# Half 0's attention in a hybrid decoder layer: values as weights, transposed probabilities streamed, division before the transposes, output collected by head pairs

## The chip, the cores and the metric

One Trainium2 chip, one NeuronCore. The metric is the device time of one execution in microseconds (us). The engines are called PE (TensorE's matmuls) and PEld (its weight loads), DVE (VectorE), ACT (ScalarE), POOL (GpSimd) and SP (SyncE). They run their own queues in order and meet at semaphores.

## The reference

One decoder layer over 1024 tokens of width 1024, all float32: a half-step SwiGLU FFN, a token mixer, a cross-attention to 256 memory tokens, and a second half-step FFN, each between two RMS norms. The mixer projects h with one matrix and has two head groups: a gated DeltaNet (4 heads of 128) and a dilated sliding-window attention (8 heads of 64). The change is in the latter:

```python
def dilated_mixer(q, k, v):
    qh, kh, vh = heads(q), heads(k), heads(v)
    slopes = 2.0 ** (-8.0 * jnp.arange(1, SWA_HEADS + 1, dtype=jnp.float32) / SWA_HEADS)
    for window, dilation in ((128, 1), (512, 4), (2048, 16)):
        o_i, lse_i = dilated_branch(qh, kh, vh, slopes, window, dilation)   # causal softmax(q k^T / 8 + alibi) v
        ...
    wts = jax.nn.softmax(jnp.stack(lses, axis=0), axis=0)
    o = jnp.einsum("gbhs,gbhsd->bhsd", wts, jnp.stack(outs, axis=0))
```

The three branches are merged by their softmax denominators. So for the first 512 tokens it is one causal softmax over at most 512 keys, if each key's score gets, beside its slope times distance, the logarithm of the number of branches that see it. The kernel does just that: the bias is made once and kept in DRAM.

## The kernel before, in words

The kernel works on two halves of 512 tokens (h is 0 or 1), each of TT = 4 tiles of P = 128 tokens. Activations are kept with channels on partitions. Every large product is made of three fp32r matmuls (high parts, and two cross terms with a low part), 128 x 128 weights against 512 columns; the high part is rounded by ACT (w_hi, line 2022), the low part subtracted by DVE (w_lo, line 2666), and SP streams raw weight blocks into a ring of three.

The order of the work is written out by hand. Each engine has a main program (the large products and what belongs to them) and a side job, a generator. After every few main matmuls PE calls `tick()`, which runs the side job's next step; the other engines call theirs at the corresponding places. Half 0's side job while its projections and the second FFN-down stage run is `mixer(0)`: its DeltaNet, and after that its attention. `MIXER[h]` is the list of its steps, the same for all engines.

Half 0's attention has UNITS = 32 units, u = 4 * head + i for query tile i. A unit has i + 1 key tiles, so the widths are 128, 256, 384 and 512. The step "att", u does on each engine:

- PE: `p_transposed(u)`, i + 1 transposes of the probabilities into the PSUM bank SB[2]; then `pv(u - 1)`, the product with the values into SB[3]; then `qk(u + 2)`, the scores into SB[0] or SB[1]. These are fp32 (the scores fp32r); an fp32 matmul shows as two records, a transpose as one.
- DVE: `smax(u + 2)`, scores plus bias and their row maximum (line 3220), the negative maximum (3227); then `fin(u - 1)`: the reciprocal of the row sum (3239) and the scaled copy of the product from SB[3] to `onat` (3241).
- ACT: `exp(u + 1)` with the row sum (2434), and `pt_copy(u)`, the transposed probabilities from SB[2] to SBUF.
- POOL: loads of queries, keys, values and biases, two heads or head pairs ahead.

`prob_of(n)` and `pt_of(n)` are rings of two. In `pv` the transposed probabilities (128 keys x 128 queries) are the stationary weights and the values (128 keys x 64) are streamed; the result has queries on partitions, in one of two places of SB[3], so `pv(u)` waits for the copy of the unit before (`out_sbuf`). The output projection needs channels on partitions. For that there is a step "pair" after every eighth unit: PE transposes the four 128 x 128 tiles of a head pair from `onat` into SB[2] (line 1837), ACT copies them to `qbT` (2479), and `p_transposed` of the following units waits for that copy (`outT_sbuf`). Two steps "conv" at the end split the DeltaNet's and the attention's output into hb_hi (ACT, 2490 and 2495) and hb_lo (DVE, 3322) for the output projection (1429 to 1431).

Main matmuls in this stretch are at lines 1561 to 1563 (`long_rows`), four accumulators A[0..3] that ACT (2055) and DVE (2703) copy out at its end. Elsewhere: 1400 to 1402 `cgran`; 1378 and 1379 `cgran_ab`, the 16 gate columns; 1724 and 1738 DeltaNet products.

Of the kernel before, what the change touches and what calls it, by code (L numbers as in the profile page):

```python
# [17 lines left out]
ACT = mybir.ActivationFunctionType  # L18
# [245 lines left out]
def hybrid_layer(nc, t):  # L264

    ctx = ExitStack()
    with ctx:
# [161 lines left out]
        def norm_ticks(r, q):  # L429
# [66 lines left out]
            "distance", "log_count", "qk_in0", "qk_in1", "v_in0", "v_in1", "bias_in0", "bias_in1", "scores", "max",  # L496
            "neg_max", "probs", "pT_psum", "pT_sbuf", "out_psum", "out_sbuf", "outT_psum", "outT_sbuf",
            "k_class", "stat_out", "stat_in", "merge_diff", "merge_exp", "out_merged", "outT_sum")}
# [841 lines left out]
        def _(pe):  # L1340
# [288 lines left out]
            def mixer(h):  # L1629
# [144 lines left out]
                def p_transposed(u):  # L1774
                    n = h * UNITS + u
                    nk = TT if h else u % TT + 1
                    pe.wait_ge(attn["probs"], n + 1)
                    if n:
                        pe.wait_ge(attn["pT_sbuf"], n)
                    if h and merged_before(u):  # L1780
                        pe.wait_ge(attn["outT_sum"], merged_before(u))
                    elif h == 0 and u >= 9:
                        pe.wait_ge(attn["outT_sbuf"], (u - 1) // 8)
                    for c in range(nk):
                        tr = pe.transpose(SB[2][:, c * P:(c + 1) * P], prob_of(n)[:, c * P:(c + 1) * P], ident[:])
                    tr.then_inc(attn["pT_psum"], 1)

                def pv(u):
                    hd, i = u // TT, u % TT
                    n = h * UNITS + u  # L1790
                    p = hd // 2
                    ch = slice((hd % 2) * AD, (hd % 2 + 1) * AD)
                    if u >= 1:
                        pe.wait_ge(attn["out_sbuf"], n)
                    pe.wait_ge(attn["pT_sbuf"], n + 1)
                    if u % 8 == 0:
                        pe.wait_ge(attn["v_in0"] if p % 2 == 0 else attn["v_in1"], 32 * h + (64 if h else 16) * (p // 2 + 1))
                    if h == 0:
                        groups = [[v_ring(h, p)[:, c, ch] for c in range(i + 1)]]
                    else:  # L1800
                        groups = [[v_ring(h, p)[:, i + c, ch] for c in range(2)], [vs_ring(p)[:, c, i, ch] for c in range(2)]]
                    for a, values in enumerate(groups):
                        for c, v in enumerate(values):
                            mm = pe.matmul(SB[3][:, out_cols(n, a)], pt_of(n)[:, (2 * a + c) * P:(2 * a + c + 1) * P], v,  # L1804
                                           start=(c == 0), stop=(c == len(values) - 1))
                    mm.then_inc(attn["out_psum"], 1)

                for what, l, k in MIXER[h]:
# [14 lines left out]
                    elif what == "att":  # L1823
# [5 lines left out]
                        if u + 2 < UNITS:  # L1829
                            if u == -2:  # L1830
                                pe.wait_ge(delta["gated"], (h + 1) * TT)
                            qk(u + 2)
                    elif what == "pair":
                        pe.wait_ge(attn["out_sbuf"], 8 * (l + 1))
                        pe.wait_ge(attn["pT_sbuf"], min(8 * (l + 1), UNITS - 1) + 1)
                        for i in range(TT):
                            tr = pe.transpose(SB[2][:, i * P:(i + 1) * P], onat_of(l)[:, 0, i, :], ident[:])
                        tr.then_inc(attn["outT_psum"], 1)
                    elif what == "merge" and k >= 2:
                        if k == 2:  # L1840
                            pe.wait_ge(attn["out_merged"], l + 1)
                            pe.wait_ge(attn["pT_sbuf"], UNITS + min(8 * l + 15, UNITS))
                        else:
                            pe.wait_ge(attn["outT_sbuf"], AH // 2 + l + 1)
                        for i in range(TT):
                            tr = pe.transpose(SB[2][:, i * P:(i + 1) * P], onat_of(l)[:, k - 2, i, :], ident[:])
                        tr.then_inc(attn["outT_psum"], 1)
# [144 lines left out]
        def _(act):  # L1992
# [393 lines left out]
            def mixer(h):  # L2386
# [62 lines left out]
                for what, l, k in MIXER[h]:  # L2449
# [27 lines left out]
                    elif what == "pair":  # L2477
                        act.wait_ge(attn["outT_psum"], l + 1)
                        act.activation(qbT[:, l, :], SB[2][:], ACT.Copy).then_inc(attn["outT_sbuf"], 1)
                    elif what == "merge" and k == 0:  # L2480
                        act.wait_ge(attn["merge_diff"], l + 1)
                        act.activation(sm[:, 2:4, :], sm[:, 2:4, :], ACT.Exp).then_inc(attn["merge_exp"], 1)
                    elif what == "merge" and k == 2:
                        act.wait_ge(attn["outT_psum"], AH // 2 + 2 * l + 1)
                        act.activation(qbT[:, l, :], SB[2][:], ACT.Copy).then_inc(attn["outT_sbuf"], 1)
# [145 lines left out]
        def _(dve):  # L2631
# [468 lines left out]
            def mixer(h):  # L3100
# [106 lines left out]
                def smax(u):  # L3207
# [18 lines left out]
                    else:  # L3226
                        dve.tensor_scalar(sm[:, 19, n % 2:n % 2 + 1], mx[:, 0:1], -(AD ** -0.5), None, ALU.mult).then_inc(attn["neg_max"], 1)

                def fin(u):
                    n = h * UNITS + u  # L3230
                    hd, i = u // TT, u % TT
                    ch = slice((hd % 2) * AD, (hd % 2 + 1) * AD)
                    if h:
                        both_parts = SB[3][:, 256 * (n % 2):256 * (n % 2) + 2 * AD].rearrange("p (a d) -> p a d", a=2)
                        dve.wait_ge(attn["out_psum"], n + 1)
                        dve.tensor_copy(onat_of(hd // 2)[:, :, i, ch], both_parts).then_inc(attn["out_sbuf"], 1)
                        return
                    dve.wait_ge(attn["probs"], n + 1)
                    link(dve.reciprocal(sm[:, 22, n % 4:n % 4 + 1], sm[:, 20, n % 4:n % 4 + 1]))
                    dve.wait_ge(attn["out_psum"], n + 1)  # L3240
                    dve.tensor_scalar(onat_of(hd // 2)[:, 0, i, ch], SB[3][:, out_cols(n)],
                                      sm[:, 22, n % 4:n % 4 + 1], None, ALU.mult).then_inc(attn["out_sbuf"], 1)

                def merge(p, k):
# [9 lines left out]
                    elif k == 1:  # L3254
# [6 lines left out]
                        parts = onat_of(p).rearrange("p a i (h d) -> p (a i h) d", h=2)  # L3261
                        dve.wait_ge(attn["out_sbuf"], UNITS + 8 * (p + 1))
                        dve.tensor_tensor(parts, parts, e_own.unsqueeze(2).to_broadcast([P, 4 * TT, AD]), ALU.mult).then_inc(attn["out_merged"], 1)
                    elif k == 3:
                        dve.wait_ge(attn["outT_psum"], AH // 2 + 2 * p + 2)
                        dve.wait_ge(attn["outT_sbuf"], AH // 2 + p + 1)
# [3 lines left out]
                for what, l, k in MIXER[h]:  # L3270
# [40 lines left out]
                    elif what == "att":  # L3311
                        u = l
                        if u + 2 < UNITS:
                            smax(u + 2)
                        if u >= 1:
                            fin(u - 1)
# [194 lines left out]
```

## Time and profile before

| what | us |
|---|---|
| median of 3 runs | 2397.37 (2395.45 to 2398.05) |
| the profiled execution | 2398.63 |
| its span, first to last instruction | 2396.8 |
| PE busy | 2352.7 (98%) |
| DVE / ACT / POOL busy | 1407.6 (59%) / 1059.5 (44%) / 513.3 (21%) |
| granted clock of PE, mean | 0.996 |

Busy time says how long an engine had an instruction in it; for PE ends are modelled and neighbours overlap, so the distance from one start to the next is what an instruction costs. An engine's idle time is given with what ended it. Half 0's attention runs from 931 to 1027 us of the span.

### The profile page before, as it was taken

The page shows a single profiled execution, that of the slowest core. Times are in us where ns is not written, and L with a number is a line of the kernel's source. Part 1 is how long each engine was busy: PE and PEld are TensorE (multiplying, and loading weights), DVE is VectorE, ACT ScalarE, POOL GpSimd, SP SyncE. Part 2 cuts the span into 40 slices and gives each one's busy share as a digit, 9 for nine tenths or more (in the row PEclk, how much of TensorE's full clock was granted, in tenths as well). Part 3 has the DMA queues.
Part 4 walks back from the last instruction along what each step waited for, and adds up shares of the span by engine and source line. Part 5 has one row for each costly group of instructions (what it writes and reads, how often), then busy time and mean ns, then how long its engine had stood idle before and what let it go on. Part 6 is the DMA issues. An engine that isn't in the chain of part 4 may idle for free.

```text
span 2396.8 us, 36179 instructions
## 1 busy us (share of the span) xinstructions
PE 2352.7 (98%) x14220; PEld 1974.5 (82%) x14220; DVE 1407.6 (59%) x2431; ACT 1059.5 (44%) x1860; POOL 513.3 (21%) x661
## 2 busy tenths in 40 slices
PE   8999999999999999999999999999999999999997
PEld 7788888888877778888788777888888888899986
DVE  6766666534676654469755565455463536799722
ACT  7544444324443323555434443686253433466511
POOL 3030000062004333222213332331020113223201
PEclk9999999999999999999999999999999999999999
DMA  8533333584533458754344432663342344644652
GB/s 270 152 107 106 118 111 106 213 296 131 167 80 98 159 199 268 210 166 125 83 124 137 125 96 63 169 166 114 103 149 88 95 144 152 207 150 150 227 214 87
DMA packets 319080, 355.19 MB, mean 148 GB/s; under 512 B 16448, under 2 KB 237888, under 8 KB 318656
## 3 DMA queue, kind: packets, MB, share of 16 engines
q1 hardware_dynamic: 282016, 264.34, 34.8%
q0 software_dynamic: 35712, 88.28, 12.1%
q8 instruction: 114, 1.87, 0.3%
q14 instruction: 54, 0.44, 0.1%
q10 hardware_dynamic: 1184, 0.27, 0.1%
HBM read 284.61 MB, written 68.22 MB: 147 GB/s over the span
## 4 chain that ended last, share of the span: by engine, by line
PE 91%; DVE 3%; ACT 2%; issue 1%; DMA 1%; POOL 1%; SPq 0%; DVEq 0%; ACTq 0%; POOLq 0%
PE acc L1400 9%; PE acc L1402 9%; PE acc L1401 9%; PE acc L1472 7%; PE acc L1473 7%; PE acc L1474 7%; PE acc L1429 5%; PE acc L1431 5%; PE acc L1430 5%; PE acc L1561 2%; PE side L1804 2%; PE acc L1563 2%; PE acc L1562 2%; PE side L1619 1%; PE side L1862 1%
## 5 line engine op out<-in xcount | busy, mean ns | idle before, releaser
L2666 DVE TENSOR_TENSOR w_lo<-w_raw,w_hi 128x1024 fp32r<-128x1024 f32 x276 | 344.9, 1250 | 350.8 <-ACT w_hi L2022 346.9
L2022 ACT ACTIVATE w_hi<-w_raw 128x1024 fp32r<-128x1024 f32 x276 | 291.6, 1057 | 335.2 <-PE acc L1431 100.9
L1400 PE MATMUL acc<-ha_hi,w_hi 128*128 128x512 f32 x800 | 323.3, 404 | 0.6 <-DVE w_lo L2666 0.6
L1402 PE MATMUL acc<-ha_hi,w_lo 128*128 128x512 f32 x800 | 313.5, 392 | 0.0
L1401 PE MATMUL acc<-ha_lo,w_hi 128*128 128x512 f32 x800 | 312.7, 391 | 0.0
L1402 PEld LDWEIGHTS acc<-ha_hi,w_lo 128*128 128x128 f32 x800 | 150.5, 188 | 32.5
L1400 PEld LDWEIGHTS acc<-ha_hi,w_hi 128*128 128x128 f32 x800 | 150.7, 188 | 29.7 <-DVE w_lo L2666 1.0
L1401 PEld LDWEIGHTS acc<-ha_lo,w_hi 128*128 128x128 f32 x800 | 150.9, 189 | 28.1
L2737 DVE TENSOR_TENSOR st_w<-st_raw,st_w 128x512 fp32r<-128x512 f32 x175 | 136.3, 793 | 54.4 <-ACT st_w L2107 53.5
L2107 ACT ACTIVATE st_w<-st_raw 128x512 fp32r<-128x512 f32 x175 | 109.4, 625 | 37.0 <-PE acc L1474 32.1
L1474 PE MATMUL acc<-s_hi,st_w 128*128 128x512 f32 x288 | 112.0, 389 | 0.0
L1473 PE MATMUL acc<-s_lo,st_w 128*128 128x512 f32 x288 | 112.0, 389 | 0.0
L1472 PE MATMUL acc<-s_hi,st_w 128*128 128x512 f32 x288 | 112.0, 389 | 0.0
L3220 DVE CUSTOM_DVE_ANT_0 arena<-side,arena 128x256 f32<-128x256 f32 (+2 forms) x96 | 40.3, 445 | 91.7 <-PE side L1771 49.9
L1118 POOL TENSOR_TENSOR arena<-arena,m_lvl 128x512 f32<-128x512 f32 x48 | 71.3, 1492 | 91.2 <-PE side L1699 79.3
L2107 ACT ACTIVATE st_w<-st_t 128x512 fp32r<-128x512 f32 x70 | 44.2, 632 | 99.9 <-PE acc L1474 59.6
L1472 PE MATMUL acc<-hb_hi,st_w 128*128 128x256 f32 (+1 forms) x276 | 87.0, 315 | 0.8 <-DVE part L2782 0.3
L1473 PE MATMUL acc<-hb_lo,st_w 128*128 128x256 f32 (+1 forms) x276 | 85.7, 311 | 0.0
L1474 PE MATMUL acc<-hb_hi,st_w 128*128 128x256 f32 (+1 forms) x276 | 85.7, 310 | 0.0
L2782 DVE TENSOR_TENSOR part<-acc,part 128x512 f32<-128x512 f32 (+1 forms) x105 | 58.4, 557 | 41.5 <-PE acc L1474 41.5
L1400 PE MATMUL acc<-hb_hi,w_hi 128*128 128x512 f32 x208 | 81.3, 391 | 0.0
L1402 PE MATMUL acc<-hb_hi,w_lo 128*128 128x512 f32 x208 | 81.0, 389 | 0.0
(529 smaller groups left out, 6073.7 us busy)
## 6 DMA issues: line engine op xcount, KB each, us to landing
act_in<-act_dram SPq DMA_DIRECT2D x88, 512.0 KB, 5.1
w_raw<-in_ffn_w_down SPq DMA_DIRECT2D x86, 512.0 KB, 3.9
act_dram<-act_out SPq DMA_DIRECT2D x66, 512.0 KB, 2.6
w_raw<-in_w_in SPq DMA_DIRECT2D x56, 512.0 KB, 3.8
w_raw<-in_ffn_w_gate SPq DMA_DIRECT2D x35, 512.0 KB, 3.8
w_raw<-in_ffn_w_up SPq DMA_DIRECT2D x35, 512.0 KB, 4.1
st_raw<-in_ffn_w_gate SPq DMA_DIRECT2D x35, 512.0 KB, 3.8
st_raw<-in_ffn_w_up SPq DMA_DIRECT2D x35, 512.0 KB, 4.9
```

Source lines behind the costliest of these rows:

```text
L1400: pe.matmul(out, hi[:, k, 0:m], xh[:, k, 0:n], start=(k == 0), stop=False)
L1401: pe.matmul(out, hi[:, k, 0:m], xl[:, k, 0:n], start=False, stop=False)
L1402: done = pe.matmul(out, lo[:, k, 0:m], xh[:, k, 0:n], start=False, stop=(k == KT - 1))
L1429: pe.matmul(out, xh[:, kk, ts], hi[:, k, :], start=(kk == 0), stop=False)
L1430: pe.matmul(out, xl[:, kk, ts], hi[:, k, :], start=False, stop=False)
L1472: pe.matmul(out, hi[:, ws], xh, start=(opens and k == 0), stop=False, skip_group_check=not opens)
L1473: pe.matmul(out, hi[:, ws], xl, start=False, stop=False, skip_group_check=not opens)
L1474: done = pe.matmul(out, lo[:, ws], xh, start=False, stop=(k == TT - 1), skip_group_check=not opens)
L2022: act.activation(hi_at(j), raw_at(j), ACT.Copy).then_inc(w_hi_ok, 1)
L2107: act.activation(st_slot(q, 0), st_source(q), ACT.Copy).then_inc(st_hi, 1)
L2666: dve.tensor_tensor(lo_at(j), raw_at(j), hi_at(j).bitcast(F32), ALU.subtract).then_inc(w_lo_ok, 1)
L2737: dve.tensor_tensor(st_slot(q, 1), st_source(q), st_slot(q, 0).bitcast(F32), ALU.subtract).then_inc(st_lo, 1)
```

## The change

For half 0 only, five things.

1. `pv`: the values (128 keys x 64 channels of the head) are the stationary weights, the transposed probabilities are streamed, and the result has channels on partitions: `SB[3][ch, i * P:(i + 1) * P]`, where ch is partitions 0 to 63 for an even head and 64 to 127 for an odd one. The eight units of a head pair fill SB[3] in the layout that `qbT` wants.
2. A row sum is now along the streamed axis, so the division comes earlier: DVE's `norm_probs(u + 1)` scales the probability row in place, ahead of `smax(u + 2)`, and `p_transposed` waits for `probs_normed`.
3. `fin` is gone in half 0, and with it the wait of `pv` for `out_sbuf`.
4. The four transposes of each step "pair" are gone; ACT copies SB[3] to `qbT` as soon as `pv` has done eight units. The step itself stays in the list.
5. The wait for that copy moves from `p_transposed` to the first `pv` of the next head pair, which overwrites SB[3].

Half 1 keeps its form; only its semaphore counts change.

```diff
                 def p_transposed(u):
                     n = h * UNITS + u
                     nk = TT if h else u % TT + 1
-                    pe.wait_ge(attn["probs"], n + 1)
+                    pe.wait_ge(attn["probs"] if h else attn["probs_normed"], n + 1)
                     if n:
                         pe.wait_ge(attn["pT_sbuf"], n)
                     if h and merged_before(u):
                         pe.wait_ge(attn["outT_sum"], merged_before(u))
-                    elif h == 0 and u >= 9:
-                        pe.wait_ge(attn["outT_sbuf"], (u - 1) // 8)
...
-                    if u >= 1:
-                        pe.wait_ge(attn["out_sbuf"], n)
+                    if h and u >= 1:
+                        pe.wait_ge(attn["out_sbuf"], u)
+                    if h == 0 and u >= 8 and u % 8 == 0:
+                        pe.wait_ge(attn["outT_sbuf"], u // 8)
                     pe.wait_ge(attn["pT_sbuf"], n + 1)
...
                     if h == 0:
-                        groups = [[v_ring(h, p)[:, c, ch] for c in range(i + 1)]]
-                    else:
-                        groups = [[v_ring(h, p)[:, i + c, ch] for c in range(2)], [vs_ring(p)[:, c, i, ch] for c in range(2)]]
+                        for c in range(i + 1):
+                            mm = pe.matmul(SB[3][ch, i * P:(i + 1) * P], v_ring(h, p)[:, c, ch], pt_of(n)[:, c * P:(c + 1) * P],
+                                           start=(c == 0), stop=(c == i))
+                        mm.then_inc(attn["out_psum"], 1)
+                        return
+                    groups = [[v_ring(h, p)[:, i + c, ch] for c in range(2)], [vs_ring(p)[:, c, i, ch] for c in range(2)]]
...
-                    elif what == "pair":
-                        pe.wait_ge(attn["out_sbuf"], 8 * (l + 1))
-                        pe.wait_ge(attn["pT_sbuf"], min(8 * (l + 1), UNITS - 1) + 1)
-                        for i in range(TT):
-                            tr = pe.transpose(SB[2][:, i * P:(i + 1) * P], onat_of(l)[:, 0, i, :], ident[:])
-                        tr.then_inc(attn["outT_psum"], 1)
...
                     elif what == "pair":
-                        act.wait_ge(attn["outT_psum"], l + 1)
-                        act.activation(qbT[:, l, :], SB[2][:], ACT.Copy).then_inc(attn["outT_sbuf"], 1)
+                        act.wait_ge(attn["out_psum"], 8 * (l + 1))
+                        act.activation(qbT[:, l, :], SB[3][:], ACT.Copy).then_inc(attn["outT_sbuf"], 1)
...
+                def norm_probs(u):
+                    dve.wait_ge(attn["probs"], u + 1)
+                    link(dve.reciprocal(sm[:, 22, u % 4:u % 4 + 1], sm[:, 20, u % 4:u % 4 + 1]))
+                    pb = prob_of(u)[:, 0:(u % TT + 1) * P]
+                    dve.tensor_scalar(pb, pb, sm[:, 22, u % 4:u % 4 + 1], None, ALU.mult).then_inc(attn["probs_normed"], 1)
+
...
-                    dve.wait_ge(attn["probs"], n + 1)
-                    link(dve.reciprocal(sm[:, 22, n % 4:n % 4 + 1], sm[:, 20, n % 4:n % 4 + 1]))
                     dve.wait_ge(attn["out_psum"], n + 1)
-                    dve.tensor_scalar(onat_of(hd // 2)[:, 0, i, ch], SB[3][:, out_cols(n)],
-                                      sm[:, 22, n % 4:n % 4 + 1], None, ALU.mult).then_inc(attn["out_sbuf"], 1)
...
                         u = l
+                        if h == 0 and 0 <= u + 1 < UNITS:
+                            norm_probs(u + 1)
                         if u + 2 < UNITS:
                             smax(u + 2)
-                        if u >= 1:
+                        if h and u >= 1:
                             fin(u - 1)
```

## Rows read from the trace of the kernel before

**Rows 1.** The page, first part: busy time, share of the span, instructions.
```profile
PE 2352.7 (98%) x14220; PEld 1974.5 (82%) x14220; DVE 1407.6 (59%) x2431; ACT 1059.5 (44%) x1860; POOL 513.3 (21%) x661
```

**Rows 2.** Waits, PE, 931 to 1032 us: total us, times, longest.
```profile
PE side L1765 <- DMA act_in<-act_dram: 0.4, 1, 0.4
PE acc L1429 <- DVE oT L2703: 0.4, 1, 0.4
```

**Rows 3.** Grouped lines, 935 to 1045 us: count, busy us, mean ns, idle before.
```profile
L1804 PE MATMUL side<-cT,arena 128*128 128x64 f32 x160 | 21.5, 265 | 0.1
...
L3241 DVE TENSOR_SCALAR arena<-side,sm 128x64 f32<-128x64 f32 x32 | 9.1, 284 | 4.1 <-PE side L1804 3.0
```

**Rows 4.** Timeline, PE, a pair step: start us, duration us, engine, line, what.
```profile
957.63 0.40 PE L1563 MATMUL acc<-w_lo,act_in 128*128 128x512 f32 x1
957.87 0.66 PE L1837 MATMUL side<-ident,arena 128*128 128x128 f32 x4
958.29 0.48 PE L1561 MATMUL acc<-w_hi,act_in 128*128 128x512 f32 x1
958.60 0.39 PE L1562 MATMUL acc<-w_hi,act_in 128*128 128x512 f32 x1
```

**Rows 5.** Timeline, PE, the value product of a 512-wide unit.
```profile
944.42 1.00 PE L1804 MATMUL side<-cT,arena 128*128 128x64 f32 x8
945.23 0.60 PE L1765 MATMUL side<-cT_r 128*128 128x384 f32 x2
```

**Rows 6.** Timeline, PE, a DeltaNet product, 128 columns loaded and streamed.
```profile
755.12 1.05 PE L1738 MATMUL side<-arena 128*128 128x128 f32 x8
755.93 0.48 PE L1400 MATMUL acc<-ha_hi,w_hi 128*128 128x512 f32 x1
756.24 0.40 PE L1401 MATMUL acc<-ha_lo,w_hi 128*128 128x512 f32 x1
```

**Rows 7.** Timelines, PE and PEld, before and after the 16 gate-column matmuls.
```profile
689.95 0.39 PE L1402 MATMUL acc<-ha_hi,w_lo 128*128 128x512 f32 x1
...
693.85 0.39 PE L1400 MATMUL acc<-ha_hi,w_hi 128*128 128x512 f32 x1
...
689.95 0.09 PEld L1378 LDWEIGHTS acc<-ha_hi,w_hi 128*16 128x16 f32 x1
```

**Rows 8.** Timelines, PE and PEld, around a group of 64*64 records.
```profile
752.01 0.40 PE L1402 MATMUL acc<-ha_hi,w_lo 128*128 128x512 f32 x1
...
753.28 0.40 PE L1401 MATMUL acc<-ha_lo,w_hi 128*128 128x512 f32 x1
...
752.34 0.54 PEld L1724 LDWEIGHTS side<-arena 64*64 64x64 f32 x8 [0.36 <-issue]
```

**Rows 9.** Grouped lines by form, DVE, whole span: scalings in SBUF.
```profile
L2982 DVE TENSOR_SCALAR stage<-stage,conv_w 128x512 f32<-128x512 f32 x24 | 11.7, 487 | 0.8
L3339 DVE TENSOR_SCALAR mprob<-mprob,sm 128x256 f32<-128x256 f32 x32 | 11.3, 354 | 1.1
```

**Rows 10.** Timelines, ACT, DVE and PE, one 512-wide unit.
```profile
962.42 0.19 ACT L2434 ACTIVATION_READ_ACCUMULATOR arena<-arena,sm 128x1 f32 x1
...
962.06 1.22 DVE L2666 TENSOR_TENSOR w_lo<-w_raw,w_hi 128x1024 fp32r<-128x1024 f32 x1
...
964.46 0.60 PE L1785 MATMUL side<-ident,arena 128*128 128x128 f32 x4
```

**Rows 11.** Timelines, ACT and PE: the pair copy, the next pair's first product.
```profile
958.57 0.60 ACT L2479 ACTIVATE cT<-side 128x512 f32<-128x512 f32 x1 [2.86 <-PE side L1837]
...
959.98 0.33 PE L1804 MATMUL side<-cT,arena 128*128 128x64 f32 x2
```

**Rows 12.** Timelines, ACT and DVE, the end of the stage.
```profile
1022.65 1.92 ACT L2490 ACTIVATE hb_hi<-zT 128x2048 fp32r<-128x2048 f32 x1
...
1026.34 0.59 ACT L2055 ACTIVATE oT<-acc 128x512 f32<-128x512 f32 x1
...
1030.98 0.69 DVE L2703 COPY oT<-acc 128x512 f32<-128x512 f32 x1
```

More of the change, by code:

```diff
@@ L496, in hybrid_layer @@
             "distance", "log_count", "qk_in0", "qk_in1", "v_in0", "v_in1", "bias_in0", "bias_in1", "scores", "max",
-            "neg_max", "probs", "pT_psum", "pT_sbuf", "out_psum", "out_sbuf", "outT_psum", "outT_sbuf",
+            "neg_max", "probs", "probs_normed", "pT_psum", "pT_sbuf", "out_psum", "out_sbuf", "outT_psum", "outT_sbuf",
             "k_class", "stat_out", "stat_in", "merge_diff", "merge_exp", "out_merged", "outT_sum")}
@@ L2483, in mixer @@
                     elif what == "merge" and k == 2:
-                        act.wait_ge(attn["outT_psum"], AH // 2 + 2 * l + 1)
+                        act.wait_ge(attn["outT_psum"], 2 * l + 1)
                         act.activation(qbT[:, l, :], SB[2][:], ACT.Copy).then_inc(attn["outT_sbuf"], 1)
@@ L3232, in fin @@
                     ch = slice((hd % 2) * AD, (hd % 2 + 1) * AD)
[L3233 to L3237, printed above, removed]
-                    dve.wait_ge(attn["probs"], n + 1)
-                    link(dve.reciprocal(sm[:, 22, n % 4:n % 4 + 1], sm[:, 20, n % 4:n % 4 + 1]))
+                    both_parts = SB[3][:, 256 * (n % 2):256 * (n % 2) + 2 * AD].rearrange("p (a d) -> p a d", a=2)
                     dve.wait_ge(attn["out_psum"], n + 1)
-                    dve.tensor_scalar(onat_of(hd // 2)[:, 0, i, ch], SB[3][:, out_cols(n)],
-                                      sm[:, 22, n % 4:n % 4 + 1], None, ALU.mult).then_inc(attn["out_sbuf"], 1)
+                    dve.tensor_copy(onat_of(hd // 2)[:, :, i, ch], both_parts).then_inc(attn["out_sbuf"], 1)
                 def merge(p, k):
@@ L3261, in merge @@
                         parts = onat_of(p).rearrange("p a i (h d) -> p (a i h) d", h=2)
-                        dve.wait_ge(attn["out_sbuf"], UNITS + 8 * (p + 1))
+                        dve.wait_ge(attn["out_sbuf"], 8 * (p + 1))
                         dve.tensor_tensor(parts, parts, e_own.unsqueeze(2).to_broadcast([P, 4 * TT, AD]), ALU.mult).then_inc(attn["out_merged"], 1)
                     elif k == 3:
-                        dve.wait_ge(attn["outT_psum"], AH // 2 + 2 * p + 2)
+                        dve.wait_ge(attn["outT_psum"], 2 * p + 2)
                         dve.wait_ge(attn["outT_sbuf"], AH // 2 + p + 1)
```

## The prediction

> **What bounds the kernel now.** I read the page's first part: TensorE's matmuls are busy 98% of the span, so what a change saves or adds on TensorE moves the end, and what it does on another engine counts only where TensorE comes to wait [rows 1]. Then the waits of TensorE in the stretch of half 0's attention (931 to 1032 us): two, 0.4 us each [rows 2]. So the attention steps there lie in line with the main products, as a sum of streaming time, with almost no latency in it. The grouped lines of that stretch give what the change touches: 160 records of the probabilities-times-values product at L1804 (80 products of two fp32 records each), and DVE's scaled copy behind each unit [rows 3]; the pair step at L1837 adds four transposes for each of four head pairs.
>
> Record durations overlap (a main matmul is shown as 0.39 us but the next starts 0.23 us later [rows 4]), so I price by distances between starts.
>
> **Part 1, the pair transposes go.** By [rows 4] the last main matmul before the step starts at 957.63, the four transposes at 957.87, the second main matmul after them at 958.60: 0.97 us. With nothing in between it would be 2 x 0.23 = 0.46 us. The step costs 0.51 us; there are 4, the last one of the same form: **-2.0 us**, all on TensorE. The tick stays (an empty one), so the spacing of the other steps is kept.
>
> **Part 2, the product turned round.** Count and type stay: 80 fp32 products, 160 records. Before, 128 columns of weights (transposed probabilities) are loaded and 64 columns streamed; after, 64 columns of weights (values) are loaded and 128 streamed. The change's shape isn't in the trace, but its neighbours are. Eight L1804 records (128x64) take from 944.42 to the next group's start at 945.23, 0.81 us [rows 5]; eight L1738 records, fp32 too, with 128 columns loaded and 128 streamed, take from 755.12 to 755.93, 0.81 us as well [rows 6]. Twice the streamed columns cost nothing there: with 64 of them the load of 128 sets the pace, and this load the change halves while the stream grows to what it was hiding behind. To the second main matmul, L1738's eight cost 756.24 - 755.12 - 0.23 = 0.89 us, 0.111 us each. I take the difference as **0**. A gain bound: the transposes of 128 columns in [rows 4] follow at (958.29 - 957.87)/4 = 0.105 us; 160 x (0.111 - 0.105) = -1.0 us.
>
> The cost bound is the use of half the array. Results now go to partitions 0-63 or 64-127, so the records become 128*64 ones among 128*128 ones, with two changes of form in each of 32 ticks. Two rows bear on this. The 128*16 and 128*8 records of the gate projection (16 of them, at L1378 and L1379) also use all rows and few columns: from the last full one at 689.95 to the next full one at 693.85 there are 17 distances in 3.90 us, 0.229 us each, the normal distance with both changes in it; and the weight load of the first one starts at 689.95, one matmul ahead, as ever [rows 7]. No price at either change. The 64*64 records do pay: their first load, 0.33 us after the last full matmul's start, isn't pulled ahead (0.36 us of "issue" before it; entry costs 0.10 us more than normal), and eight records with 64 streamed columns cost 753.28 - 752.01 - 0.46 = 0.81 us, 0.101 us each, where streaming needs half of the 0.105 us of 128 columns [rows 8]. If the new records behaved so, each would take 0.101 + 0.053 = 0.154 us, 0.043 us more than now, and 160 of them 6.9 us. The change keeps all 128 rows, as the 128*16 records do, so I take the 0 of that row and keep 6.9 us as the upper end.
>
> The Trainium skill speaks against the change here: TensorEngine Tiling (Array Packing), section "Key Properties", says "Mode switching requires drain" and lists 128-row forms of 64 and 32 columns as modes of their own. By that rule every tick would pay twice; the trace agrees for the 64*64 records and not for the 128*16 ones. Its outcome is the first rival below.
>
> **Part 3, division ahead of the transposes.** DVE's per-unit work changes from a reciprocal and a 64-wide scaled copy out of PSUM (0.28 us) [rows 3] to the same reciprocal and a scaling of the whole probability row in SBUF. The nearest rows are the memory attention's 128x256 scaling, 0.35 us, and a 128x512 one in SBUF, 0.49 us [rows 9]; so about 0.28, 0.35, 0.42 and 0.49 us for the four row lengths, 32 units x 0.10 us more on average, 3 us on an engine that is half idle: 0. What matters is its place. The new order is exp on ACT, scaling on DVE, then the transposes on TensorE, and DVE blocks on exp with its next row maximum and the stream's w_lo split queued behind. The tightest place I found is that of a 512-wide unit with a w_lo split in between [rows 10]: exp's sum is read out by 962.42 + 0.19 = 962.6; DVE's split stands at 962.06 to 963.28, and starts 0.3 to 0.4 us earlier once the old scaled copy before it is gone, so it ends by 962.9; the scaling (0.49 us) with its reciprocal (an estimate of 0.15 to 0.25 us with handing over, no more than the 0.28 us of the small copy) ends by 963.65; TensorE's transposes of that unit start at 964.46. 0.8 us is left. DVE's next row maximum slips by some 0.4 us behind it, but its own transposes come a whole tick after 964.46. In ticks without a split the margin is larger. I cost this part at **0**; a scaling of twice the length (1 us) would use up the 0.8 us, and each of the ten or so splits of the stage would then cost TensorE some 0.2 us: up to +2 us.
>
> TensorE also loses a wait: the product no longer waits for the last unit's copy out, since each query tile of a head pair has its own place in SB[3]. In its stead the first product of the next pair waits for ACT's copy of SB[3], and behind it on TensorE stand that tick's scores and all main products. The copy stood idle 2.86 us for the pair transposes and ran from 958.57 for 0.60 us; the next pair's first product starts at 959.98 [rows 11]. Even at its old time it leaves 0.8 us, and it can now start up to 2.9 us sooner: 0.
>
> **Part 4, the end of the stage.** The second 0.4 us wait is TensorE's for an accumulator that DVE copies at 1030.98 to 1031.68; DVE comes late to it because it converts the attention output first, which ACT prepares only after the last pair copy and its own accumulator copy at 1026.34 [rows 12]. ACT's conversion before these ends at 1022.65 + 1.92 = 1024.6, and the last pair copy (0.60 us) can follow at once instead of waiting for transposes; so ACT's copy at 1026.34 can start up to 0.9 us earlier and DVE with it, while TensorE arrives only 0.5 us earlier (the pair step). The wait goes: **-0.4 us**, bounds 0 and -0.4.
>
> **Sum.** -2.0 + 0 + 0 - 0.4 = -2.4, and -0.3 for the product records (between 0 and their gain bound of -1.0, nearer to 0 as [rows 5, 6] are alike). Total -2.7 us. The profiled execution took 2398.63 us (span 2396.8, 1.8 us around it), 1.3 us over the median 2397.37 of three runs, so I apply the difference to the median: **2394.7 us**. After the stage TensorE is again nearly gapless, so I expect what is saved to reach the end.
>
> **Rivals.** (1) The column form drains, as the 64*64 records of [rows 8] do: +6.9 us from the 32 ticks x 5 records, 2394.7 + 6.9 = 2401.6 us, slower than before. It decides from 0.017 us a record on (2.7 us / 160); for it speak [rows 8], against it [rows 7]. 10%. (2) The saving is taken back by a transfer: one of the two waits is put down to a DMA, so landings are not far off; if a later one sets a stage's start, TensorE only waits longer there and the end stays at 2397.4 us. Against it: 0.4 us in 101 us is all it waits for a DMA [rows 2]. 10%. (3) The longer softmax chain stalls the transposes in the ticks with a split: +2 us, 2396.7 us; against it the 0.8 us of room. 7%. (4) The records reach the gain bound (0.7 us more than the sum has) and the median falls by half the spread of the three runs (1.3 us): 2392.7 us. 5%.
>
> **Chances.** The forecast holds 68%. About 0.2% (4.8 us) is what measurement can tell from no change. Faster by more needs twice what I can find: 4%. Slower by more, past 2402.2 us, needs rival 1 above its price or with rival 3: 7%. Within: 89%. The range for 8 in 10 reaches down to rival 4 and up to rival 1: 2392.8 to 2401.7.
>
> **What would show it.** Right: no L1837, L1804's successor 160 records of 128*64, eight of them again 0.81 us apart from the next group, their first weight load one matmul ahead, no idle time of TensorE on the scaling or on SB[3]'s copy, and busy time some 2.6 us smaller in this pass. Wrong: an "issue" gap before the loads at each product group and 0.10 us more at entry (rival 1); TensorE waiting for DVE's scaling (rival 3); the stage shorter but the end unmoved (rival 2).

## The result, and the profile after

| what | before | after |
|---|---|---|
| median of 6 runs, us | 2397.71 (2395.45 to 2399.18) | 2405.03 (2403.96 to 2405.74) |
| ratio, with its 95% interval | | 1.0028 (1.0018 to 1.0038) |
| span of the profiled execution, us | 2396.8 | 2403.7 |
| half 0's attention, us | 95.41 | 103.34 |

The changed kernel is slower by 7.3 us. The last row is the distance from the last main matmul ahead of the first score step to the first matmul of the output projection (L1429), read off TensorE's timeline: 931.62 to 1027.03 before, 931.92 to 1035.26 after. That stage grew by 7.93 us, so the loss is all in it; outside it the profiled execution is 1.0 us shorter.

The page of the changed kernel, first part, beside [rows 1]: 16 transposes fewer, and yet TensorE is busy 8.1 us longer.

```profile
PE 2360.8 (98%) x14204; PEld 1972.7 (82%) x14204; DVE 1413.0 (59%) x2431; ACT 1060.0 (44%) x1860; POOL 513.2 (21%) x661
```

Waits of TensorE from 925 to 1045 us: none is listed, where [rows 2] have two. Yet the stage is longer, so the loss must be in the distances between the instructions. Waits of DVE, 935 to 1030 us (total us, times, longest): it sits idle before the scaling (L3228) in 23 units until ACT's exp is done, as the prediction said it would, and TensorE doesn't wait for it.

```profile
DVE arena L3217 <- PE side L1765: 22.9, 23, 1.9
DVE sm L3228 <- ACT arena L2431: 16.7, 23, 0.9
```

Grouped lines, 935 to 1060 us, the successors of [rows 3]:

```profile
L1800 PE MATMUL side<-arena,cT 128*64 128x128 f32 x160 | 24.3, 283 | 0.0
...
L1800 PEld LDWEIGHTS side<-arena,cT 128*64 128x64 f32 x160 | 16.6, 136 | 6.4 <-issue 6.4
...
L3230 DVE TENSOR_SCALAR arena<-arena,sm 128x128 f32<-128x128 f32 (+3 forms) x32 | 12.7, 396 | 1.1
```

The matmul row looks harmless: 283 ns instead of 265, and 0.0 us of idle time. The weight loads tell more: 6.4 us of "issue" before 160 of them, 0.2 us for each of 32 groups.

The last product of the stage is the best place to look, as it is the only thing between two main matmuls. Timelines of TensorE (start, duration), before, then its weight loads:

```profile
1021.32 0.39 PE L1563 MATMUL acc<-w_lo,act_in 128*128 128x512 f32 x1
1021.55 1.00 PE L1804 MATMUL side<-cT,arena 128*128 128x64 f32 x8
1022.36 0.48 PE L1561 MATMUL acc<-w_hi,act_in 128*128 128x512 f32 x1
1022.67 0.39 PE L1562 MATMUL acc<-w_hi,act_in 128*128 128x512 f32 x1
...
1021.32 1.09 PEld L1804 LDWEIGHTS side<-cT,arena 128*128 128x128 f32 x8
```

The same place after, with two of its weight loads:

```profile
1029.41 0.40 PE L1563 MATMUL acc<-w_lo,act_in 128*128 128x512 f32 x1
1029.73 1.09 PE L1800 MATMUL side<-arena,cT 128*64 128x128 f32 x8
1030.75 0.50 PE L1561 MATMUL acc<-w_hi,act_in 128*128 128x512 f32 x1
1031.09 0.39 PE L1562 MATMUL acc<-w_hi,act_in 128*128 128x512 f32 x1
...
1029.73 0.85 PEld L1800 LDWEIGHTS side<-arena,cT 128*64 128x64 f32 x8 [0.36 <-issue]
1030.75 0.19 PEld L1561 LDWEIGHTS acc<-w_hi,act_in 128*128 128x128 f32 x1 [0.17 <-issue]
```

Before, the first load starts at 1021.32, together with the main matmul ahead of it; after, it starts only with its own matmul, and so does the first main load behind the group. In starts: entry 0.32 us instead of 0.23, product to next matmul 1.02 instead of 0.81, exit 0.34 instead of 0.31; together 0.33 us more.

The records by themselves say where that time lies. Timelines of windows so narrow that the first record, or all but the last, are left out, so that a line begins with the second of the eight (x7) and with the last (x1): after, and then the same two in the kernel with all 128 columns loaded (first of the experiments below), where the first record starts at 1016.11:

```profile
1029.89 0.93 PE L1800 MATMUL side<-arena,cT 128*64 128x128 f32 x7
1030.55 0.27 PE L1800 MATMUL side<-arena,cT 128*64 128x128 f32 x1
...
1016.22 0.94 PE L1800 MATMUL side<-arena,cT 128*128 128x128 f32 x7
1016.89 0.28 PE L1800 MATMUL side<-arena,cT 128*128 128x128 f32 x1
1016.92 0.48 PE L1561 MATMUL acc<-w_hi,act_in 128*128 128x512 f32 x1
```

From the second record to the last are six distances, 0.11 us each in both forms. With 64 columns it is the ends that are longer: 0.32 us to the first record instead of 0.23, 0.16 to the second instead of 0.11, and 0.20 from the last one to the main matmul instead of 0.03. So the records themselves aren't dearer.

I then took the cost of every tick in the same way (from the last main matmul before it to the second after it, less two normal distances, 0.457 us). Each tick has transposes, a value product and scores, but the last three, which have no scores; two of these (not in the table) go from 0.78 to 1.11 and from 1.11 to 1.44, and the third is the product alone:

| value records in the tick | 2 | 4 | 6 | 8 | 8, product alone |
|---|---|---|---|---|---|
| before, us | 0.91 | 1.00 | 1.35 | 1.35 | 0.89 |
| after, us | 1.24 | 1.34 | 1.68 | 1.69 | 1.22 |

The surplus is 0.33 or 0.34 us in every one, for 2 records as for 8, for even heads (partitions 0 to 63) as for odd ones: 32 x 0.33 = 10.6 us. The balance of the stage:

| term | us |
|---|---|
| 32 product groups x 0.33 | +10.6 |
| four pair steps gone, 0.51 x 3 + 0.45 (the last one) | -2.0 |
| two ticks in which TensorE waited before, at 949.11 (1.65 instead of 1.00) and 983.99 (1.35 instead of 1.00), now at 1.34 like the others | -1.0 |
| new wait ahead of L1429 | +0.3 |
| sum, and measured | +7.9, +7.93 |

The first of the two ticks is the one of the DMA wait in [rows 2]. The second is in no list of waits and shows only in the distances; the lines of the kernel before tell what it was:

```profile
984.46 0.28 DVE L3241 TENSOR_SCALAR arena<-side,sm 128x64 f32<-128x64 f32 x1
...
984.79 0.32 PE L1804 MATMUL side<-cT,arena 128*128 128x64 f32 x1
```

The product starts 0.05 us after DVE's scaled copy of the unit before has ended (984.74): it is the wait of `pv` for `out_sbuf`, which part 3 of the change takes away. Behind the stage after is 1.3 us shorter than before; 0.4 of it is the other wait of [rows 2], the rest I can't place.

The new wait is at the very end. Timelines of the changed kernel, TensorE and DVE:

```profile
1034.74 0.39 PE L1563 MATMUL acc<-w_lo,act_in 128*128 128x512 f32 x1
1035.26 0.47 PE L1429 MATMUL acc<-w_hi,hb_hi 128*128 128x512 f32 x1
...
1032.87 2.29 DVE L3320 TENSOR_TENSOR hb_lo<-zT,hb_hi 128x2048 fp32r<-128x2048 f32 x1 [2.61 <-ACT hb_hi L2487]
```

DVE's split of the DeltaNet output ends at 1032.87 + 2.29 = 1035.16, and L1429 starts at 1035.26, 0.52 us after its predecessor instead of 0.23. Before, that split ran 1024.60 to 1026.89 and L1429 started at 1027.03 at the normal distance: it was already last but one, by 0.14 us.

### The profile page after: what moved, and what is told of

Its sections match the earlier page's. It is cut to its first block, busy times and chain, and to the rows that moved or that the text cites. A ratio compares the mean times of both kernels' runs of the same rounds, so it can differ in the third digit from the quotient of the medians.

```text
span 2403.7 us, 36083 instructions
## 1 busy us (share of the span) xinstructions
PE 2360.8 (98%) x14204; PEld 1972.7 (82%) x14204; DVE 1413.0 (59%) x2431; ACT 1060.0 (44%) x1860; POOL 513.2 (21%) x661
## 4 chain that ended last, share of the span: by engine, by line
PE 93%; DVE 3%; ACT 2%; issue 1%; POOL 0%; DMA 0%; SPq 0%; DVEq 0%; ACTq 0%; POOLq 0%
PE acc L1400 10%; PE acc L1402 9%; PE acc L1401 9%; PE acc L1472 7%; PE acc L1474 7%; PE acc L1473 7%; PE acc L1429 5%; PE acc L1431 5%; PE acc L1430 5%; PE acc L1561 2%; PE acc L1563 2%; PE acc L1562 2%; PE side L1619 1%; PE side L1859 1%; PE side L1807 1%; PE side L1783 1%
```

## The experiments

Two theories stood against each other. A: going into and out of a form with fewer columns than 128 costs TensorE 0.33 us per group, whatever the number of records. B: the records are dearer each, or it is the neighbours (transposes ahead, scores behind) that make the price. The single records above speak for A; the runs test both. A later question was why the 16 gate columns of [rows 7], on which the prediction stood, don't pay.

**All 128 columns.** The changed kernel, with the product loading both heads' values, so that the form stays 128*128; the other head's 64 result partitions are thrown away, and ACT copies the head's own half after each fourth unit.

```diff
-                    if h == 0 and u >= 8 and u % 8 == 0:
-                        pe.wait_ge(attn["outT_sbuf"], u // 8)
+                    if h == 0 and u >= TT and u % TT == 0:
+                        pe.wait_ge(attn["outT_sbuf"], u // TT)
...
-                            mm = pe.matmul(SB[3][ch, i * P:(i + 1) * P], v_ring(h, p)[:, c, ch], pt_of(n)[:, c * P:(c + 1) * P],
+                            mm = pe.matmul(SB[3][:, i * P:(i + 1) * P], v_ring(h, p)[:, c, :], pt_of(n)[:, c * P:(c + 1) * P],
...
+                            act.wait_ge(attn["out_psum"], u)
+                            act.activation(qbT[ch, done // 2, :], SB[3][ch, :], ACT.Copy).then_inc(attn["outT_sbuf"], 1)
```

> The changed kernel, but each value product loads all 128 columns of the head pair's values (both heads) and writes all 128 partitions; ACT copies the head's own 64 partitions to qbT after every fourth unit, before the next head overwrites them. Everything else of the change stays: turned product, division first, no pair transposes. Switch theory (entering and leaving the 64-column form costs 0.33 us a tick, whatever it holds): the product's ticks return to 0.91, 1.00, 1.35 and 1.35 us over the main matmuls, 32 x 0.33 = 10.6 us under the changed kernel, so about 2394.4 us, faster than before by some 3 us. Streaming theory (128 streamed columns cost more than 64): stays at 2405. Chain theory (the division delays the transposes): stays at 2405.

Measured: 2396.98 us against 2397.61 of before beside it, ratio 0.9997 (0.9988 to 1.0006): no faster than before, 2.6 us above what was expected, and 8 us under the changed kernel when each is compared with the kernel before beside it. The ticks are back at 0.91, 1.00, 1.35 and 1.35 to 0.02 us, but for the one with a DMA wait. Timeline of TensorE, the eight value records of a tick, and the end of the stage with DVE:

```profile
951.72 1.05 PE L1800 MATMUL side<-arena,cT 128*128 128x128 f32 x8
952.53 0.60 PE L1765 MATMUL side<-cT_r 128*128 128x384 f32 x2
...
1020.25 2.29 DVE L3322 TENSOR_TENSOR hb_lo<-zT,hb_hi 128x2048 fp32r<-128x2048 f32 x1 [3.18 <-ACT hb_hi L2489]
...
1022.65 0.47 PE L1429 MATMUL acc<-w_hi,hb_hi 128*128 128x512 f32 x1 [1.39 <-issue]
```

From 951.72 to 952.53 are 0.81 us, as in [rows 5] and [rows 6]: 128 streamed columns cost no more than 64, as predicted. On TensorE only the number of columns differs from the changed kernel, and the place of the wait for ACT's copy, for which no idle time is listed; so the 10.6 us are the price of the 64 columns. What of the -2.0 us is left? The stage takes 94.59 us, 0.82 less than before: -2.0 for the pair steps and -0.35 for the tick at 983.99, against +0.1 where a DMA wait is back (1.73 us in that tick instead of 1.65) and +1.55 at L1429, which starts 1.78 us behind its predecessor; 0.1 us of the sum stays unplaced. Here the list puts that DMA wait down to the queries (cT_r<-q_dram). The split again ends just ahead of L1429, at 1022.54, and the trace puts 1.39 us of TensorE's idle time down to "issue" only.

**Division first.** The kernel before, with part 3 alone: `norm_probs` ahead of the transposes, and a plain copy of the product in `fin`.

```diff
-                    pe.wait_ge(attn["probs"], n + 1)
+                    pe.wait_ge(attn["probs"] if h else attn["probs_normed"], n + 1)
...
+                        if h == 0 and 0 <= u + 1 < UNITS:
+                            norm_probs(u + 1)
```

> The kernel before with one part of the change alone: the probabilities are scaled before the transposes, and the copy out of PSUM is a plain copy; product, pair transposes and waits as before. Switch theory: 2397.7 within 1 us, no wait of TensorE on the scaling. Chain theory: slower by several us, up to the 7 us of the change, with TensorE idle before the transposes.

Measured: 2397.76 us, ratio 1.0002 (0.9993 to 1.0011). Waits of TensorE, 931 to 1032 us:

```profile
PE side L1804 <- DVE arena L3245: 0.3, 1, 0.3
```

The other one listed is that of [rows 2] for L2703. None is for the scaled probabilities. DVE is busy 9.5 us longer, and what reaches TensorE of it is small: in two ticks the product comes just behind the plain copy (L3245), which costs 0.2 us in each (1.19 and 1.59 us, where before has 1.00 and 1.35), and it is the wait for `out_sbuf` that the changed kernel no longer has. The division isn't the cause.

**Two more switches per tick.** The changed kernel, with the first score matmul (128*128) put between the first value product and the others in the 21 ticks that have several key tiles and scores to come.

```diff
+                    values(0)
+                    scores(0)
+                    for c in range(1, i + 1):
+                        mm = values(c)
+                    mm.then_inc(attn["out_psum"], 1)
+                    scores(1).then_inc(attn["scores"], 1)
```

> The changed kernel with the first score matmul (128 columns of weights) put between the first and the other value records of a tick, in 21 of the 32 ticks, so that these go in and out of the 64-column form twice. No work is added. Switch theory: 21 x 0.33 = 6.9 us more than the changed kernel, 2412 us. Record theory (160 half-width records at 0.066 us more each): no change, 2405 us.

Measured: 2412.84 us, ratio 1.0066 (1.0052 to 1.0080), 7.8 us over the changed kernel (4 runs). The ticks with 4, 6 and 8 records went up by another 0.29, 0.33 and 0.33 us, the one with 2, which can't be split, stayed at 1.24. Seven of each make 6.7 us, and the stage grew by 6.6 us (109.90 against 103.34); the rest of the 7.8 us isn't in it. Timeline of TensorE:

```profile
945.94 0.39 PE L1563 MATMUL acc<-w_lo,act_in 128*128 128x512 f32 x1
...
946.37 0.43 PE L1764 MATMUL side<-arena,cT 128*64 128x128 f32 x2
946.74 0.44 PE L1769 MATMUL side<-cT_r 128*128 128x384 f32 x1
947.11 0.87 PE L1764 MATMUL side<-arena,cT 128*64 128x128 f32 x6
947.90 0.44 PE L1769 MATMUL side<-cT_r 128*128 128x384 f32 x1
```

The same eight records in two groups pay twice. That fixes the unit of the price: one stay in the 64-column form, not one record.

**Product ahead of the transposes.** The changed kernel with `pv(u - 1)` as the first thing of the tick, directly behind a main matmul.

```diff
+                        if h == 0 and u >= 1:
+                            pv(u - 1)
...
-                        if u >= 1:
+                        if h and u >= 1:
```

> The changed kernel with the value product ahead of the tick's transposes, so that it follows a main fp32r matmul and precedes a transpose. Switch theory: 2405 within 1 us, the same 0.33 us a tick. Neighbour theory (what costs is half-width records beside transposes or beside the scores): another price a tick, some us less or more.

Measured: 2404.26 us, ratio 1.0030 (1.0020 to 1.0039); ticks 1.21, 1.27, 1.63, 1.63, so the surplus is 0.27 to 0.30 us. Another neighbour changes the price by 0.03 to 0.07 us and doesn't take it away (if the order alone would cost nothing with 128 columns, which no run shows). This half of theory B is out too.

**Width and type.** The kernel before with extra work: ahead of each of eight granules of the gate stage, eight products of 128 streamed columns whose results are overwritten, with 16, 32, 64 or 128 columns of weights, once as fp32 (two records each) and once as fp32r (one).

```diff
+                    c = (16, 32, 64, 128)[i - START["gdn0"] - 4]
+                    for k in range(KT):
+                        pe.matmul(out[0:c, 0:P], hi[:, k, 0:c].bitcast(F32), xh[:, k, 0:P].bitcast(F32), start=(k == 0), stop=(k == KT - 1))
...
+                    c = (16, 32, 64, 128)[i - START["gdn0"] - 8]
+                    for k in range(KT):
+                        pe.matmul(out[0:c, 0:P], hi[:, k, 0:c], xh[:, k, 0:P], start=(k == 0), stop=(k == KT - 1))
```

> The kernel before with eight extra matmuls of 128 streamed columns ahead of each of eight gate-stage products, whose results are overwritten: in fp32 with 16, 32, 64 and 128 columns of weights, then in fp32r with the same four widths. From the last full matmul before to the second one after: theory W (any narrower column form pays at entry and exit): 16, 32 and 64 columns each some 0.3 us over 128, in both types. Theory T (only fp32 pays, which would explain the free 128*16 records of fp32r): a step in fp32 between 64 and 128 columns, none in fp32r. Theory N (32-column forms are free, 64-column forms pay): a step for 64 alone in both types. The work is in addition to the reference's.

One run, 2407.60 us against 2397.92, with the extra work in it; only the groups are compared. Timeline of TensorE: fp32 with 16 and with 128 columns, fp32r with 64 and with 128; last the weight loads of fp32 and of fp32r with 64 columns.

```profile
646.32 0.39 PE L1410 MATMUL acc<-ha_hi,w_lo 128*128 128x512 f32 x1
646.64 1.92 PE L1400 MATMUL acc<-ha_hi,w_hi 128*16 128x128 f32 x16
...
648.83 0.40 PE L1409 MATMUL acc<-ha_lo,w_hi 128*128 128x512 f32 x1
...
668.91 0.39 PE L1410 MATMUL acc<-ha_hi,w_lo 128*128 128x512 f32 x1
669.14 1.95 PE L1400 MATMUL acc<-ha_hi,w_hi 128*128 128x128 f32 x16
...
671.15 0.40 PE L1409 MATMUL acc<-ha_lo,w_hi 128*128 128x512 f32 x1
...
688.17 0.39 PE L1410 MATMUL acc<-ha_hi,w_lo 128*128 128x512 f32 x1
688.40 0.64 PE L1404 MATMUL acc<-ha_hi,w_hi 128*64 128x128 f32 x8
...
689.16 0.40 PE L1409 MATMUL acc<-ha_lo,w_hi 128*128 128x512 f32 x1
...
694.18 0.39 PE L1410 MATMUL acc<-ha_hi,w_lo 128*128 128x512 f32 x1
694.41 1.00 PE L1404 MATMUL acc<-ha_hi,w_hi 128*128 128x128 f32 x8
...
695.54 0.40 PE L1409 MATMUL acc<-ha_lo,w_hi 128*128 128x512 f32 x1
...
661.67 1.72 PEld L1400 LDWEIGHTS acc<-ha_hi,w_hi 128*64 128x64 f32 x16 [0.35 <-issue]
...
688.17 0.72 PEld L1404 LDWEIGHTS acc<-ha_hi,w_hi 128*64 128x64 f32 x8
```

| cost of the group, us (less 0.457) | 16 columns | 32 | 64 | 128 |
|---|---|---|---|---|
| fp32, 16 records | 2.05 | 2.06 | 2.08 | 1.78 |
| fp32r, 8 records | 0.53 | 0.53 | 0.53 | 0.90 |

As fp32 every narrower form pays 0.27 to 0.30 us for its group, 16 columns no less than 64. As fp32r no price shows: the first load of such a group starts with the main matmul ahead (688.17), and all three groups are cheaper than the one with 128 columns. So the gate columns of [rows 7] went free because they are fp32r, not because they use all rows.

**Gate columns as fp32.** The cross-check: the kernel before, with its own 128*16 and 128*8 matmuls of [rows 7] in fp32.

```diff
-                    pe.matmul(out[0:16, :], both_parts[:, k, 0:16], xh[:, k, :], start=(k == 0), stop=False)
+                    pe.matmul(out[0:16, :], both_parts[:, k, 0:16].bitcast(F32), xh[:, k, :].bitcast(F32), start=(k == 0), stop=False)
```

> The kernel before with the 16 gate-column matmuls (128*16 and 128*8) in fp32 instead of fp32r, same operands. Theory T: the load of the first is no longer pulled ahead (an issue gap) and about 0.1 us more at entry and 0.2 at exit. Theories W and N: entry as in the kernel before, 0.23 us after the last full matmul. The fp32 records themselves cost more in either case.

One run, 2417.84 us against 2397.92; two records of 512 columns for one make up nearly all of that, so only the ends of the group say something. TensorE, the two ends, and the first weight load:

```profile
689.86 0.39 PE L1402 MATMUL acc<-ha_hi,w_lo 128*128 128x512 f32 x1
690.18 1.03 PE L1378 MATMUL acc<-ha_hi,w_hi 128*16 128x512 f32 x2
...
703.06 1.02 PE L1379 MATMUL acc<-ha_lo,w_hi 128*8 128x512 f32 x2
...
704.35 0.40 PE L1401 MATMUL acc<-ha_lo,w_hi 128*128 128x512 f32 x1
...
690.17 0.11 PEld L1378 LDWEIGHTS acc<-ha_hi,w_hi 128*16 128x16 f32 x2 [0.35 <-issue]
```

0.32 us at entry and a load that isn't pulled ahead, at the very place where [rows 7] have neither. An estimate of the whole stay's price: inside the group the 16 products start 0.859 us apart ((703.06 - 690.18)/15), so of the 14.49 us from 689.86 to 704.35 the products are 13.74 and two normal distances 0.46, which leaves 0.29 us for a stay of 32 records.

**All columns, and the end of the stage relieved.** The 1.4 us at L1429 were still open. ACT's conversion of the DeltaNet output stood behind the last head's copy and its wait for the last product; here it comes ahead of the copy, and DVE's split waits for the last product by itself.

```diff
-                            act.wait_ge(attn["out_psum"], (h + 1) * UNITS)
+                            act.wait_ge(attn["out_psum"] if h else attn["max"], (h + 1) * UNITS)
...
+                        if h == 0 and l == 0:
+                            dve.wait_ge(attn["out_psum"], UNITS)
```

> full_cols with its end mended: the last head's copy comes after the DeltaNet conversion instead of ahead of it, and that conversion's first half (hb_hi) waits for the last row maximum, not for the last value product; only its second half (hb_lo) still waits for that product. Theory of the tail (TensorE's 1.4 to 1.5 us wait ahead of the output projection in full_cols, and 0.3 us in the changed kernel, are this conversion, which the pair transposes used to cover): the wait goes, 1.5 us under full_cols, about 3 us under the kernel before, 2394.6 us. Rival: something else feeds the projection late and the wait stays.

> full_cols once more, on the chip of full_cols_tail, to set the two side by side. Switch theory with the tail: 1 to 1.5 us under the kernel before and as much above full_cols_tail. If all my prices but the switch were wrong, it would be no faster than before.

Measured: 2395.5 us (11 runs) against 2397.84 of before (21 runs), ratio 0.9991 (0.9982 to 0.9999), an interval that only just leaves out no change; the version with all columns beside it again took 2397.18, ratio 0.9999 (0.9990 to 1.0008), with its 1.4 us of idle time again. Between these two lie 1.7 us, where 1 to 1.5 were expected. Against the kernel before both gave less than forecast: 2.3 us instead of about 3, and 0.7 us instead of 1 to 1.5. Timelines of the relieved version, TensorE and DVE:

```profile
1025.14 0.39 PE L1563 MATMUL acc<-w_lo,act_in 128*128 128x512 f32 x1
1025.49 0.47 PE L1429 MATMUL acc<-w_hi,hb_hi 128*128 128x512 f32 x1
...
1023.09 2.29 DVE L3328 TENSOR_TENSOR hb_lo<-zT,hb_hi 128x2048 fp32r<-128x2048 f32 x1 [1.77 <-ACT hb_hi L2493]
```

L1429 now comes 0.35 us behind its predecessor, 0.12 more than normal. So it was this conversion that held TensorE. The version takes 2.3 us less than the kernel before. Its stage takes 93.67 us, 1.74 less than before: -2.0 and -0.35 as above, +0.1 at L1429, +0.2 for the DMA wait, which falls in an earlier tick (1.86 us instead of 1.00 there, and 1.00 instead of 1.65 at its old place) and +0.3 in the first score tick (0.53 instead of 0.22).

## Why the prediction was wrong

**The bound and Part 1: right.** TensorE stayed the bound, and the four pair steps gave their 2.0 us.

**Part 2: wrong, and it decided.** Two things were asked in it. The rate of the records came as said: eight take 0.81 us with 128 columns loaded, whether 64 or 128 are streamed, shown by the kernel with all columns; and 0.11 us each inside a group of the new form. The step that failed is "so I take the 0 of that row". Two rows stood at hand, 128*16 ones without a price and 64*64 ones with one, and I chose by the number of rows, which the new records share with the first. But the first are fp32r, and the new ones share their type, fp32, with the second. Width and type measured one by one show that the type decides: fp32 pays at 16, 32 and 64 columns, fp32r at none. In place of that 0 the runs showed 0.33 us in each of the 32 ticks, 10.6 us.

**Rival 1: right in its mechanism, wrong in its size.** It took the whole difference of the 64*64 group as a price per record, 0.043 us x 160 = 6.9 us. The price is one of a group: 0.33 us x 32 = 10.6 us, as the ticks with 2 to 8 records and the product cut in two show. The same rows had both readings: 8 x 0.043 = 0.34 us is the price of one group of eight. And single records told them apart: of the eight in [rows 8] the first starts at 752.34, the second at 752.45 and the others 0.058 us apart, so the prediction's 0.101 us each was seven short distances with a price at both ends. With 5 records in a mean tick, the reading per record comes out a third too low. With 10.6 added to the sum's -2.7 the forecast would have been +7.9 us, 2405.3, above the range's end, against 2405.03 measured. That this fits so well is in part luck: the sum has -0.4 for a wait and -0.3 for the records, where the stage shows -1.0 and +0.3 for other waits.

The rule quoted from the Trainium skill, TensorEngine Tiling (Array Packing), section "Key Properties", that a mode switch drains, fits the price that fp32 pays here (0.27 to 0.34 us in and out) and not fp32r (no price at 16, 32 or 64 columns); that the engine drains is in no row. So its warning was the better guide for this change, and the row set against it was of the other type.

**Part 3: right for the division and for SB[3], and one gain overlooked.** Division first costs nothing that can be measured (1.0002), and no wait of TensorE is for the scaled probabilities. But the prediction priced the wait for `out_sbuf` that it took away at nothing, and it was worth 0.35 us, in the tick at 983.99: with all columns, where TensorE comes early again, that tick stays at 1.00 us. The wait for SB[3] is right too: in after, ACT copies the first pair at 958.42 for 0.60 us, and the next pair's first product comes in the tick that begins at 961.30.

**Part 4: right in what it took, wrong in what comes next.** The 0.4 us wait for L2703 is gone in after, and in both versions with all columns. What I left out is that the pair step covered the DeltaNet conversion, which ended 0.14 us ahead of L1429: 0.3 us of new wait in after, 1.55 where the ticks are short, 0.1 once it is moved forward. Likewise the DMA wait: I took it as standing; it goes where TensorE comes later and returns (+0.1, +0.2 us) where it comes earlier, which is rival 2 in small. This wait and the one of part 3 were worth 1.0 us, of which the list of waits had shown 0.4.

**The -0.3 us for the records** can't be told from 0: the ticks of the version with all columns agree with those of before to 0.02 us.

Not settled: why a narrow form pays as fp32 alone. The load that isn't pulled ahead goes with the price in each place, but no run takes the one without the other. The profiled execution of the version with all columns was 5.4 us shorter than that of before, where the medians lie 0.6 us apart and its stage explains 0.8. 3.6 us of it lie ahead of the stage, where the two kernels do the same, and it goes with the granted clock: of this version's 11 runs the three with a mean of 0.997 took 2393.2 to 2395.2 us, the four with 0.994 took 2398.2 to 2398.9. So only medians are used above for such totals. Why the clock differs from run to run stays open.

## What to carry to other kernels

Where the nearest rows of a trace disagree, list every way in which they differ from the new case, element type as well as shape (here the type decided), and when that leaves it open forecast the dearer one. Price a change of form by the group that stays in it, from the last full matmul before it to the second after it, and multiply by groups, not by records. Loading columns that are thrown away can be the cheaper form: here, in fp32, 128 columns of which 64 are used save 8 us over 64 alone. And whatever ended just ahead of a stage's first instruction becomes the bound when the work that covered it goes.

## What the hardware showed unexpectedly

- A group of fp32 matmuls with 16, 32 or 64 columns of weights among 128*128 fp32r ones costs 0.27 to 0.34 us over the same group with 128 columns, whatever the width and the number of records (2 to 16, and 32 by an estimate); the time lies at the group's two ends, and with 128 streamed columns the records between start 0.11 us apart, as in the full form; its first load shows 0.35 us of "issue" instead of starting one matmul ahead.
- fp32r groups in the same forms show no such price, and are cheaper: eight with 128 streamed columns cost 0.53 us (0.066 each) at 16 to 64 columns of weights and 0.90 us (0.11 each) at 128.
- An fp32 record takes 0.11 us with 128 columns loaded, whether 64 or 128 are streamed.
- None of this shows in the list of waits; distances between starts, and the "issue" time of the weight loads, are the rows that have it.
